# One layer of a bidirectional RWKV-7 / GLA / MoE trunk: inputs and gate products of the opening stage in another order

## The reference, cut to what matters

```
mod = silu(cond) @ w_ada + b_ada            # 1024 -> 6 x 1024, for c_ctx and for c
sh1, sc1, ga1, sh2, sc2, ga2 = split(mod)
h   = rmsnorm(x, norm1_g) * (1 + sc1) + sh1
... = split(h @ w_in)                       # r k v, low-rank inputs, q_g k_g v_g, og, lgk_f lgk_b
gk  = log_sigmoid(lgk[d] @ gla_gk2[d] + gla_gk_b[d]) / 16     # lgk[d]: 16 columns of w_in, d = 0, 1
y_rw, y_gla = RWKV-7 scan (both directions), chunked GLA scan (both directions)
x  += ga1 * (concat(y_rw, y_gla) @ w_out)
x  += ga2 * hier_moe(rmsnorm(x, norm2_g) * (1 + sc2) + sh2)   # 16 experts, two per token
```

## Time and profile before

| | |
|---|---|
| median of 3 runs | 982.75 us (978.35 to 985.03) |
| the profiled execution | 982.82 us |
| its span | 981.0 us |
| mean granted TensorE clock | 0.948 of full |
| busy: PE / DVE / ACT / POOL | 873.4 / 560.7 / 334.1 / 146.8 us |
| span until the slab qk is done with | 103.2 us |

### The profile page before, as it was taken

The page is one execution under the profiler, slowest core; times in us unless marked ns, Lnnn a source line. Parts: engine busy times, 40 slices in busy tenths (PEclk is TensorE's granted clock), DMA queues, the critical chain, the costliest instruction groups (busy, mean ns, idle before and its releaser), DMA issues.

```text
span 981.0 us, 21494 instructions
## 1 busy us (share of the span) xinstructions
PE 873.4 (89%) x8900; PEld 535.9 (55%) x8900; DVE 560.7 (57%) x933; ACT 334.1 (34%) x585; POOL 146.8 (15%) x296
## 2 busy tenths in 40 slices
PE   2799999999999988778888987899994799999996
PEld 0445445655555544567777776745574354444442
DVE  1524016689967798756556664697326145554467
ACT  3222111133023758376556653312210122232223
POOL 6000101112000011334232231000001001000041
PEclk9899999999899989799999999999985799999998
DMA  9810433014224400211212211591009589999957
GB/s 330 325 64 1 134 131 102 22 69 150 87 86 172 172 1 11 40 30 31 41 32 38 49 33 49 177 363 44 33 11 342 193 276 369 369 370 368 340 125 228
DMA packets 119760, 142.46 MB, mean 145 GB/s; under 512 B 49964, under 2 KB 85224, under 8 KB 119272
## 3 DMA queue, kind: packets, MB, share of 16 engines
q1 hardware_dynamic: 110824, 116.55, 36.2%
q0 software_dynamic: 3744, 13.63, 4.5%
q10 hardware_dynamic: 5088, 10.82, 2.9%
HBM read 122.99 MB, written 18.00 MB: 144 GB/s over the span
## 4 chain that ended last, share of the span: by engine, by line
PE 78%; DVE 12%; issue 4%; ACT 3%; DMA 2%; SPq 1%; ACTq 0%; DVEq 0%; POOLq 0%
PE bank L1947 70%; PE bank L1951 8%; DVE rk_r L1406 2%; DMA region<-in_w_ada_dram 2%; ACT region L933 1%; DMA rk_r<-h_rows_dram,slot_tokens 1%; DVE region L1406 1%; DVE rk_r L1407 1%; DVE cl_b L1319 1%; DVE cl_b L1865 1%; DVE region L1936 0%; ACT w_sb L933 0%; DVE region L1350 0%; DVE region L1932 0%; ACT ada_row_buffers L933 0%
## 5 line engine op out<-in xcount | busy, mean ns | idle before, releaser
L1947 PE MATMUL bank<-region 64*64 64x64 f32 (+3 forms) x3904 | 400.6, 299 | 16.1 <-issue 7.1
L1947 PEld LDWEIGHTS bank<-region 64*64 64x64 f32 (+1 forms) x3904 | 232.5, 149 | 170.0 <-issue 159.2
L933 ACT ACTIVATE region<-bank 128x256 f32<-128x256 f32 (+3 forms) x216 | 98.1, 454 | 352.0 <-PE bank L1947 256.6
L1951 PE MATMUL bank<-ident,region 128*128 128x128 f32 (+2 forms) x403 | 67.3, 301 | 27.7 <-DMA scratch<-in_gla_gk_dram 12.6
L1947 PE MATMUL bank<-region,rk_r 128*128 128x512 f32 x176 | 80.3, 610 | 0.8 <-issue 0.8
L1951 PEld LDWEIGHTS bank<-ident,region 128*128 128x128 f32 (+2 forms) x403 | 49.6, 154 | 43.9 <-issue 34.3
L1917 DVE TENSOR_SCALAR region<-region 128x256 f32<-128x256 f32 x16 | 4.7, 294 | 100.6 <-ACT region L933 100.6
L1406 DVE SCALAR_TENSOR_TENSOR rk_r<-region,vec,rk_r 128x512 f32<-128x512 f32 x64 | 50.3, 786 | 12.3 <-ACT rk_r L933 10.2
L1947 PEld LDWEIGHTS bank<-region,rk_r 128*128 128x128 f32 x176 | 33.7, 196 | 39.7 <-issue 38.6
L908 POOL DMA_INDIRECT rk_r<-h_rows_dram,slot_tokens x16 | 15.2, 952 | 245.6 <-PE bank L1951 132.0
L1588 DVE TENSOR_TENSOR region<-bank,region 128x256 f32<-128x256 f32 x60 | 25.5, 425 | 41.5 <-PE bank L1947 40.2
(11 more groups left out here) (277 smaller groups left out, 1151.9 us busy)
## 6 DMA issues: line engine op xcount, KB each, us to landing
region<-in_moe_w_dram SPq DMA_DIRECT2D x38, 1024.0 KB, 10.3
region<-in_w_ada_dram SPq DMA_DIRECT2D x12, 2048.0 KB, 8.7
region<-in_w_in_dram SPq DMA_DIRECT2D x6, 2048.0 KB, 7.8
cl_b<-in_moe_w_dram SPq DMA_DIRECT2D x10, 1024.0 KB, 12.7
expert_rows_dram<-yg_b ACTq DMA_DIRECT2D x14, 512.0 KB, 6.8
region<-late_condition_dram SPq DMA_DIRECT2D x3, 1024.0 KB, 9.7
a_rows_dram<-region SPq DMA_DIRECT2D x20, 128.0 KB, 2.9
region<-inverse_rows_dram SPq DMA_DIRECT2D x20, 128.0 KB, 3.0
```

Source lines behind the costliest of these rows:

```text
L933: return act.activation(out, in_, func, **kw)
L1947: return pe.matmul(out, lhsT, rhs, start=start, stop=stop)
L1951: return pe.transpose(out, in_, ident[0:n, 0:n])
```

## The change

- SP: `w_lgk` and the two parts of `gla_gk2` are sent after the fourth slab and counted on `s_lgk` (48); `rw_w2`, `rw_a2` and the zeros are sent after the sixth slab, the first two counted on a new `s_rank`, for which TensorE waits before the first low-rank product (`low_rank("w", 0)`).
- ScalarE waits for each tile of x by itself; it squares three tiles, then exponentiates the conditioning, then squares the last two. It has three columns of h (0, 2, 4), and moves out q0 before it works on the gates.
- VectorE normalises x first of all, and has five columns of h (1, 3, 5, 7, 6).
- TensorE: `hl` 0 to 3 come before the turn of slice 0, `hl` 4 to 7 and `hc` after slice 2. The gate products take the columns in the order `COLS_DONE` (1, 0, 3, 2, 5, 7, 4, 6), both directions for each column in turn. Unit q0 stands between the gate products and those with `gla_gk2`, and these go direction by direction within a column block.

```diff
-        jobs += [("ada", 0), ("ada", 1), ("adaT", 0)]
-        jobs += [("hl", k) for k in range(KT)] + [("hc", 0), ("hc", 1)]
-        jobs += [("ada", 2), ("adaT", 1), ("ada", 3), ("adaT", 2), ("adaT", 3)]
+        jobs += [("ada", 0), ("ada", 1)] + [("hl", k) for k in range(4)] + [("adaT", 0)]
+        jobs += [("ada", 2)] + [("hl", k) for k in range(4, KT)] + [("hc", 0), ("hc", 1)]
+        jobs += [("adaT", 1), ("ada", 3), ("adaT", 2), ("adaT", 3)]
...
+        jobs += [("lgkl",), ("lgkc",)] + unit("q0")
+        jobs += [("gkl", d, i) for i in range(GC) for d in range(2)] + [("gkc",)]
...
-            sp.dma_start(w2_sb[:, :], rw_w2[0].rearrange("d k n -> (d k) n")).then_inc(s_small, 16)
-            sp.dma_start(a2_sb[:, :], rw_a2[0].rearrange("d k n -> (d k) n")).then_inc(s_small, 16)
-            sp.dma_start(gk2_sb[0:GKL, :], gla_gk2[0, 0]).then_inc(s_small, 16)
-            sp.dma_start(gk2_sb[32:32 + GKL, :], gla_gk2[0, 1]).then_inc(s_small, 16)
             for i in range(RING):
                 slab_dmas(sp, i)
-            sp.dma_start(w_lgk, w_in_v[:, :, oLGK:oLGK + 2 * GKL]).then_inc(s_lgk, 16)
             for i in range(RING, NS1):
                 if i == 2 * RING:
+                    sp.dma_start(w_lgk, w_in_v[:, :, oLGK:oLGK + 2 * GKL]).then_inc(s_lgk, 16)
+                    sp.dma_start(gk2_sb[0:GKL, :], gla_gk2[0, 0]).then_inc(s_lgk, 16)
+                    sp.dma_start(gk2_sb[32:32 + GKL, :], gla_gk2[0, 1]).then_inc(s_lgk, 16)
+                if i == 3 * RING:
+                    sp.dma_start(w2_sb[:, :], rw_w2[0].rearrange("d k n -> (d k) n")).then_inc(s_rank, 16)
+                    sp.dma_start(a2_sb[:, :], rw_a2[0].rearrange("d k n -> (d k) n")).then_inc(s_rank, 16)
                     sp.wait_ge(s_zero_src, 1)
...
-            wait_result(act, "rows")
-            tell(A(stmp, vec[:, vcond:vcond + 2 * KT], ACT.Exp, scale=-1.0), s_cond)
-
-            act.wait_ge(s_x, 16 * NT)
             act.wait_ge(s_eps, 1)
             for t in range(NT):
+                if t == NT - 2:
+                    wait_result(act, "rows")
+                    tell(A(stmp, vec[:, vcond:vcond + 2 * KT], ACT.Exp, scale=-1.0), s_cond)
+                act.wait_ge(s_x[t], 16)
                 own(A(kk_b[:, 0:D], x_sb[:, t], ACT.Square, accum_out=ssum[:, t:t + 1]))
...
-            for k in range(0, KT, 2):
+            for k in COLS[0]:
...
+            dve.wait_ge(s_xn, 1)
+            normalise_x(range(NT))
             ada_rows_out(0)
             ada_rows_out(1)
+            h_lat_out(1)
+            h_lat_out(3)
             ada_turned_out(0)
-            dve.wait_ge(s_xn, 1)
-            normalise_x(range(NT))
...
-            pe.wait_ge(s_small, 16 * 16)
+            pe.wait_ge(s_small, 16 * 12)
...
             ada_rows(0)
             ada_rows(1)
+            pe.wait_ge(s_const, 1)
+            pe.wait_ge(s_xnr, 1)
+            for k in range(4):
+                h_lat(k)
+            ada_turn(0)
             ada_rows(2)
+            for k in range(4, KT):
+                h_lat(k)
+            h_ctx(0)
+            h_ctx(1)
             ada_turn(1)
             ada_rows(3)
             ada_turn(2)
...
-                for d in range(2):
-                    for k in range(KT):
-                        if d == 0 and key == "lgkl":
-                            pe.wait_ge(s_hT[k % 2], k // 2 + 1)
-                        ins = mm(b[32 * d:32 * d + GKL, 0:n], w_lgk[:, k, d * GKL:(d + 1) * GKL], hT[:, k, sl], start=k == 0, stop=k == KT - 1)
+                for n_, (j, m) in enumerate(COLS_DONE):
+                    k = COLS[j][m]
+                    if key == "lgkl":
+                        pe.wait_ge(s_hT[j], m + 1)
+                    for d in range(2):
+                        ins = mm(b[32 * d:32 * d + GKL, 0:n], w_lgk[:, k, d * GKL:(d + 1) * GKL], hT[:, k, sl], start=n_ == 0, stop=n_ == KT - 1)
                 finish(ins)
+            w = slab("qk")
+            project("q0", w, 0)
```

More of the change, by code:

```diff
@@ L303, in trunk_program @@
         jobs = [("rows",)]
-        jobs += [("ada", 0), ("ada", 1), ("adaT", 0)]
-        jobs += [("hl", k) for k in range(KT)] + [("hc", 0), ("hc", 1)]
-        jobs += [("ada", 2), ("adaT", 1), ("ada", 3), ("adaT", 2), ("adaT", 3)]
+        jobs += [("ada", 0), ("ada", 1)] + [("hl", k) for k in range(4)] + [("adaT", 0)]
+        jobs += [("ada", 2)] + [("hl", k) for k in range(4, KT)] + [("hc", 0), ("hc", 1)]
+        jobs += [("adaT", 1), ("ada", 3), ("adaT", 2), ("adaT", 3)]
         chan = ["q0", "q1", "g0", "g1"]
         tail = [f"r{i}" for i in range(RC)] + [f"k{i}" for i in range(RC)] + [f"v{i}" for i in range(RC)] + ["lw", "la", "lg"]
-        jobs += [("lgkl",), ("lgkc",)]
-        jobs += [("gkl", d, i) for d in range(2) for i in range(GC)] + [("gkc",)]
         def unit(n):
             return [("pl", n), ("pc", n)]
+        jobs += [("lgkl",), ("lgkc",)] + unit("q0")
+        jobs += [("gkl", d, i) for i in range(GC) for d in range(2)] + [("gkc",)]
         def turn(n):
@@ L328, in slot @@
             return out
-        for n in chan:
+        for n in chan[1:]:
             jobs += unit(n)
@@ L421, in trunk_program @@
         s_small = sem("small_loads")
-        s_x = sem("x_loads")
+        s_x = [sem(f"x_load{t}") for t in range(NT)]
+        s_rank = sem("low_rank_weights")
         s_const = sem("constants")
@@ L469, in trunk_program @@
         s_hT = [sem(f"h_columns{j}") for j in range(2)]
+        COLS = [(0, 2, 4), (1, 3, 5, 7, 6)]
+        COLS_DONE = [(1, 0), (0, 0), (1, 1), (0, 1), (1, 2), (1, 3), (0, 2), (1, 4)]
         s_bon = sem("bonus_inputs")
@@ L964, in _, with qk_out @@
                 tell(A(hT[:, k, 0:P], hT[:, k, 0:P], ACT.Identity, scale=gscv[:, 0, k, 0:1], bias=modv[:, k, 0:1]), s_hT[0])
+            def qk_out(n, i):
+                sc = HD ** -0.5 if n[0] == "q" else 1.0
+                copy_out(qk_g[:, i, P:T], ("pl", n), scale=sc)
+                copy_out(qk_g[:, i, 0:P], ("pc", n), bank(("pc", n))[:, 0:P], scale=sc)
+            qk_out("q0", 0)
             act.wait_ge(s_lgx, 1)
@@ L970, in _ @@
             tell(A(glt, glt, ACT.Ln, bias=1.0), s_lgt)
[L972 to L975, removed]
+            for n, i in (("q1", 1), ("g0", GC), ("g1", GC + 1)):
+                qk_out(n, i)
             def gla_exps(p):
@@ L1351, in normalise_x, with h_lat_out @@
                     own(ins) if t < NT - 1 else tell(ins, s_xnr)
+            def h_lat_out(k):
+                wait_filled(dve, "hl", k)
+                out_of(dve.tensor_copy(hT[:, k, P:T], bank(("hl", k))[:, :]), "hl", k)
+            dve.wait_ge(s_xn, 1)
+            normalise_x(range(NT))
             ada_rows_out(0)
             ada_rows_out(1)
+            h_lat_out(1)
+            h_lat_out(3)
             ada_turned_out(0)
-            dve.wait_ge(s_xn, 1)
-            normalise_x(range(NT))
-            for k in range(1, KT, 2):
-                wait_filled(dve, "hl", k)
-                out_of(dve.tensor_copy(hT[:, k, P:T], bank(("hl", k))[:, :]), "hl", k)
+            ada_rows_out(2)
+            h_lat_out(5)
+            h_lat_out(7)
             wait_filled(dve, "hc", 1)
             out_of(dve.tensor_copy(hT[:, 4:8, 0:P], bank(("hc", 1))[:, :].rearrange("p (k t) -> p k t", k=4)), "hc", 1)
-            ada_rows_out(2)
             ada_turned_out(1)
@@ L1367, in _ @@
             tell(STT(gscv[:, 0], modv[:, KT:2 * KT, :], 1.0, bc(vec[:, vn1:vn1 + KT], 2, 2), ALU.add, ALU.mult), s_g1)
-            for k in range(1, KT, 2):
+            for k in COLS[1]:
                 if k == 1:
                     wait_result(dve, "hc", 0)
+                elif k == 6:
+                    wait_result(dve, "hl", 6)
                 own(TS(hT[:, k, P:T], hT[:, k, P:T], gscv[:, 0, k, 1:2], modv[:, k, 1:2], ALU.mult, ALU.add))
@@ L1378, in _ @@
                 out_of(dve.tensor_copy(lgkT[32:32 + GKL, sl], bank(key)[32:32 + GKL, 0:n]), *key)
-            for d in range(2):
-                for i in range(GC):
+            for i in range(GC):
+                for d in range(2):
                     wait_filled(dve, "gkl", d, i)
@@ L2014, in ada_group, with h_lat @@
                     ada_turn(n)
[L2015 to L2019, removed]
-            for k in range(KT):
+            def h_lat(k):
                 b = open_bank("hl", k)
@@ L2024, in _, with h_ctx @@
                 finish(ins)
-            for j in range(2):
+            def h_ctx(j):
                 b = open_bank("hc", j)
@@ L2029, in _ @@
                 finish(ins)
+            ada_rows(0)
+            ada_rows(1)
+            pe.wait_ge(s_const, 1)
[3 more added lines that the diff above has]
+            ada_turn(0)
             ada_rows(2)
+            for k in range(4, KT):
+                h_lat(k)
+            h_ctx(0)
+            h_ctx(1)
             ada_turn(1)
@@ L2043, in project @@
                     finish(ins)
-            pe.wait_ge(s_lgk, 16)
+            pe.wait_ge(s_lgk, 48)
```

(5 more changed lines are left out.)

4 lines of the change are left out of this document (2 added, 2 removed).

## The result

| | before | after |
|---|---|---|
| median (range) | 980.89 us (978.35 to 985.03, 4 runs) | 964.09 us (961.32 to 970.37, 4 runs) |
| ratio after / before | | 0.9846, 95% interval 0.981 to 0.9882 |
| profiled execution, span | 982.82, 981.0 us | 966.3, 964.6 us |
| the `w_ada` slab after qk goes out (end of the opening) | 103.17 | 88.17 |
| from there to the end of the span | 877.8 | 876.4 |

What follows compares the result with a forecast made beforehand. TensorE was taken as the bound (78% of the chain, DMA 2%). Gain 7.2, first column 0.5, gate products 5.2, stall 0.8 and lower clock 0.9 sum to 14.6 us from 982.8: 968.2, range 961 to 975.

Steps and rivals of the forecast that it cites:

- Everything behind moves as one piece: From 66 us on, all work moves earlier together with the opening, since later DMA issues wait for TensorE too.
- The gain 7.2 us earlier: Opening, instruction on gsc: made at 38.4 instead of 45.62, 7.2 us earlier (6 to 8.6).
- it is, by a microsecond: Slab 3 must be in at 34.2, 4.2 us before the gain; claimed to be met, with 33 taken.
- Slab 2 at 27.0 to 28.2, slab 3 at 32.4 to 34.5: Expected landing times in us of the third and fourth w_ada slabs in the opening; 33 taken for slab 3.
- First column 0.5: Before the gate products: VectorE makes the first column right behind the gain, saving 0.5 us (0 to 1).
- Gate products 5.2: Gate stage: both column groups side by side take 10.1 us instead of 15.3, saving 5.2 us.
- stall: Before the products with gla_gk2: q0 covers VectorE's copying of the gate inputs, saving 0.8 us.
- Both column groups at once: Gate stage: the two directions' products overlap fully, 8.6 us plus 1.5 at the lower clock.
- the factor of 1.6: Rival, gate stage: two column groups overlap only partly, 12.2 us for the stage, 970.3 in all; chance 0.07.
- Lower clock after the gates 0.9: Between 65.93 and 75.24: 1.6 to 1.8 us lost to the clock may stay away; half taken, 0.9.
- The low-rank weights and zeros cost nothing: Loads sent later, behind vg: all landed by 52 and hidden, since they are used only later.
- my case for a slower kernel: Rival, gate weights landing late: gain gone if they land at 53, kernel 1% slower from 63; chance 0.03.

Runs made afterwards that it cites:

- e2: The changed kernel with the loads back in the order of before; median 968.18 us, ratio to before 0.9858, gain at 40.76.
- e9: The changed kernel with extra unused products in three TensorE waits (before slab 0, between slabs 0 and 1, before the gate products); median 956.91 us, ratio to before 0.9768.
- e1: The changed kernel with the gate products again direction by direction; gate stage 15.6 us, median 970.3 us, ratio to before 0.989.
- e6: The kernel before with one edit, gate products taking both directions for each column in turn; gate stage 10.9 us, median 976.86 us, ratio to before 0.9956.
- e8: The changed kernel with two extra unused products while TensorE waits for the first column of h; gate stage 8.7 us, median 960.9 us, ratio to before 0.9803.
- e5: The changed kernel with q0 again behind the products with gla_gk2; opening ends at 91.6, median 969.13 us, ratio to before 0.9878.

## Why the prediction was right

Right in sum (14.6 us forecast; 15.1 by the ratio, 15.0 in the opening of the profiled pair) and in most steps. The time itself came out 4 us under the 968.2, of which 1.9 are the base: I subtracted from 982.8, and the median of the four runs before is 980.9.

- *Everything behind moves as one piece*: yes. TensorE's instructions lie 15.0 us earlier from the end of the opening to 262 us of the kernel before, where a wait of 2.2 us is followed by different lengths of lower clock (6.8 and 3.4 us).
- *The gain 7.2 us earlier*: 7.4, and this agreement is luck, because errors of 3 us each way nearly cancel. TensorE's work came 3.0 us sooner than summed: slab 1 landed at 21.16, not 21.6 (the bytes taken from in front of slab 0 gave 1.8 us, not 1.4), its products took 1.9 us, not 3.6, and the transposes, taken to lose 0.9 to the clock, lost nothing. Against it stand 2.8 us of waits that I had put at nothing, 1.8 for slab 2 and 1.0 for slab 3. So **"it is, by a microsecond" failed**: slab 3 was to be in at 33, landed at 34.04 and was waited for. I had summed TensorE's work as without holes, where the chain after is DMA to 34.04. e2 shows that as cause: the gain follows slab 3 by 4.2 us there too.
- *Slab 2 at 27.0 to 28.2, slab 3 at 32.4 to 34.5*: 27.6 and 34.04, inside, but 33 was too early. By my own rate two slabs behind 21.16 are in at 32.0. An estimate from the rates is that the hole at 20 to 22 adds 1.0 us, (387 - 184) x 2 / 387, and what passes beside slab 3 the other 1.0; the lower rate at 32 to 34 (284 and 354) makes up 0.4 of that. I had read the 220 GB/s of the earlier trace rows as `w_lgk` alone. It did land there, at 23.3, but there, too, slab 2 had been sent only 1.6 us before slab 1 landed (21.43, 23.05), and the changed kernel has rates as low at this place with no `w_lgk` near; so the 220 hold something of both. e9 closes the hole, and slab 3 is in at 33.0.
- *SP's issue of `w_lgk` takes 5.6*: it took 0.58, and the issue of the first `gla_gk2` part behind it 5.46. So the 5.6 were not due to the small pieces; the qk slab went out at 30.2 and landed at 40.1, in time.
- *First column 0.5*: 1.76 to 1.29. *Gate products 5.2*: 15.3 and the stall to 10.4 is 5.7, of which 0.8 is the *stall* step, so 4.9 here; 8.6 + 1.5 was 0.3 short. e1 and e6 confirm the mechanism, 5.1 and 5.2.
- *Both column groups at once* against the factor of 1.6, my estimate for two tiles from the 2.38 that the Trainium skill measured for three (TensorE: Matmul & The Clock Gate, Part 3): by it the stage would be 12.2 us with the lower clock, 10.7 without. It was 10.4, and in e8, at full clock throughout, 8.7, where the rows gave 8.6. For these products the measurement decides against that estimate.
- *Lower clock after the gates 0.9*, the even chance: it stayed away, and what lies behind the gate stage is 1.5 us shorter (39.7 to 38.2). The staying away was a draw: it came in e1 and e8 with q0 in the same place. In e5 the old place of q0 cost 3.9 us, against the 0.8 + 0.9 given to it, but with a lower stretch twice as long as before.
- *The low-rank weights and zeros cost nothing*: right; TensorE waits for nothing of them. The last zeros had landed at 50.7. The gate weights, my case for a slower kernel, were in at 33.3 and the last of the three loads on `s_lgk` at 34.8, 4.7 us before the first gate product.

The parts do not add up by themselves. Undoing them one at a time costs 5.1 (gates), 2.5 (loads) and 5.5 (norm) at their own points. Done alone on the kernel before, the gates keep theirs (5.2), the loads bring 1.1.

## What to carry to other kernels

When two paths end in one instruction, work out both to their end and take the later one, with the margin between them: here the path of the engine shrank by more than its margin, and the slabs became the bound, which also made the edit of the loads worth twice what it brings alone (2.5 and 1.1 us). Issue products on different 32-column groups in turn, not one group after the other: here that was 10.4 us for 15.6. Send the next slab early enough: 1.7 us ahead of the landing of the one before left the DMA engines a hole of 1.0 us. A wait just ahead of a chain of products can cost more than its length when the clock falls after it. Useless products in the waits took the opening from 88.2 to 85.6 us in one run (e9); in the gate stage alone they gave 1.7 us there and none at the end of the opening (e8).

## What the runs showed of the hardware that was not expected

Small products of 128 columns, whose result nobody reads, made slab 0's products 1.92 us instead of 3.50 (e9). In the timeline of e9 the sixteen records ahead of slab 0 took 0.24 us each, the twenty-eight behind it 0.12, so the change of speed came before slab 0's products:

```profile
11.75 3.78 PE L1960 MATMUL bank<-ident 128*128 128x128 f32 x16
...
17.93 3.39 PE L1960 MATMUL bank<-ident 128*128 128x128 f32 x28
```

The granted clock of the profile shows 1.00 in both, and in the slow products of slab 0 in every run, so there the durations have to be read. How long the lower level then lasts behind the same step differs from run to run, 3.4 or 6.8 us (before and e5), and in e1 and e8 it came where in the changed kernel it did not; no run here settles what decides that.
